# The FFN of two layers in four parts of 1024 of d_ff, written out, where it was two parts of 2048 in loops

## Time and profile before

| what | value |
| --- | --- |
| median of three runs | 2458.11 us (2457.42 to 2458.26) |
| span of the profiled execution | 2455.7 us |
| PE busy | 2437.2 us (99%) |
| DVE busy | 1321.1 us (54%) |
| ACT busy | 941.3 us (38%) |
| POOL busy | 292.5 us (12%) |
| DMA, mean | 106 GB/s |

### The profile page before, as it was taken

How to read it: one execution, slowest core, us unless ns; L and a number is a source line. 1 busy time by engine, 2 the same in 40 slices (tenths; PEclk the granted TensorE clock), 3 DMA queues, 4 the chain that set the end, 5 groups by cost and what they waited for, 6 DMA issues and landing times.

```text
span 2455.7 us, 31484 instructions
## 1 busy us (share of the span) xinstructions
PE 2437.2 (99%) x12348; PEld 1991.3 (81%) x12348; DVE 1321.1 (54%) x1761; ACT 941.3 (38%) x1359; POOL 292.5 (12%) x237
## 2 busy tenths in 40 slices
PE   9999999999999999999999999999999999999998
PEld 7877988889876888888988888877778788888886
DVE  7764732434966563243543437769995386343322
ACT  4345532333445453232432235532335554322321
POOL 1231000001122100000111123400000121111101
PEclk9999999999999999999999999999999999999999
DMA  4312222222231222222222235643342143222222
GB/s 165 142 44 69 86 103 103 86 103 103 78 129 35 103 86 100 89 103 94 79 103 102 93 103 174 206 164 116 142 149 83 63 152 129 100 88 102 78 98 81
DMA packets 46253, 259.64 MB, mean 106 GB/s; under 512 B 5504, under 2 KB 6016, under 8 KB 23232
## 3 DMA queue, kind: packets, MB, share of 16 engines
q1 hardware_dynamic: 43712, 248.42, 29.0%
q0 software_dynamic: 640, 5.51, 0.6%
q10 hardware_dynamic: 1792, 4.20, 0.5%
HBM read 240.27 MB, written 16.78 MB: 105 GB/s over the span
## 4 chain that ended last, share of the span: by engine, by line
PE 91%; DVE 6%; ACT 2%; issue 1%; DMA 0%; DVEq 0%; SPq 0%; ACTq 0%
PE gemm L451 74%; DVE out_sb L1599 2%; PE gemm L733 1%; DVE w_lo L401 1%; PE gemm L744 1%; PE gemm L735 1%; PE gemm L698 1%; PE gemm L699 1%; PE gemm L696 1%; PE turned L1135 1%; PE mixed L1147 1%; PE score L1124 1%; PE gemm L626 1%; PE gemm L627 1%; PE gemm L635 1%
## 5 line engine op out<-in xcount | busy, mean ns | idle before, releaser
L401 DVE TENSOR_TENSOR w_lo<-w_raw,w_hi 128x2048 fp32r<-128x2048 f32 (+2 forms) x207 | 439.2, 2122 | 480.7 <-ACT w_hi L393 480.3
L451 PE MATMUL gemm<-h_hi,w_hi 128*128 128x512 f32 x1744 | 691.2, 396 | 2.6 <-DVE w_lo L401 2.2
L451 PE MATMUL gemm<-h_hi,w_lo 128*128 128x512 f32 x1744 | 679.9, 390 | 0.0
L451 PE MATMUL gemm<-h_lo,w_hi 128*128 128x512 f32 x1744 | 679.2, 389 | 0.0
L393 ACT ACTIVATE w_hi<-w_raw 128x2048 fp32r<-128x2048 f32 (+3 forms) x217 | 381.9, 1760 | 345.5 <-PE gemm L451 302.8
L451 PEld LDWEIGHTS gemm<-h_hi,w_hi 128*128 128x128 f32 x1744 | 327.7, 188 | 81.8 <-issue 9.1
L451 PEld LDWEIGHTS gemm<-h_hi,w_lo 128*128 128x128 f32 x1744 | 327.3, 188 | 69.6
L451 PEld LDWEIGHTS gemm<-h_lo,w_hi 128*128 128x128 f32 x1744 | 327.8, 188 | 65.7 <-issue 1.0
L451 PE MATMUL gemm<-f_hi,w_hi 128*128 128x512 f32 x448 | 174.3, 389 | 0.0
L451 PE MATMUL gemm<-f_lo,w_hi 128*128 128x512 f32 x448 | 174.3, 389 | 0.0
L451 PE MATMUL gemm<-f_hi,w_lo 128*128 128x512 f32 x448 | 174.3, 389 | 0.0
(11 more groups left out here) (462 smaller groups left out, 3816.0 us busy)
## 6 DMA issues: line engine op xcount, KB each, us to landing
w_raw<-in_w SPq DMA_DIRECT2D x171, 1024.0 KB, 4.8
w_raw<-in_w SPq DMA_DIRECT2D x16, 768.0 KB, 4.2
w_raw<-in_w SPq DMA_DIRECT2D x16, 640.0 KB, 3.8
w_raw<-in_w SPq DMA_DIRECT2D x18, 512.0 KB, 3.6
trig_kept<-made SPq DMA_DIRECT2D x16, 512.0 KB, 5.7
trig<-trig_kept SPq DMA_DIRECT2D x16, 512.0 KB, 6.2
bias_t<-in_att_bias SPq DMA_DIRECT2D x2, 1536.0 KB, 8.1
decay_t<-in_c_decay SPq DMA_DIRECT2D x2, 1536.0 KB, 8.1
```

The costliest lines, as they stand in the source:

```text
L401: dve.tensor_tensor(flat(w_lo, b), flat(w_raw, b), flat(w_hi, b).bitcast(F32), ALU.subtract).then_inc(S["w_rest"], 1)
L451: mm = pe.matmul(dst, lhs, rhs, start=b.first and k == 0 and j == 0, stop=b.last and k == b.kt - 1 and j == 2)
```

## The change

The FFN goes in four parts of 1024 of d_ff: 4 up pieces, then 4 down pieces. `f_hi` and `f_lo` hold 8 tiles instead of 16. Each down output tile is one piece with a PSUM group of its own; the first part's 8 are copied to `out_sb` by ACT, those of the other three are added there by DVE (`added_down`). All loops of the FFN are written out. `last_in_halves` takes the one last piece instead of two. The spare place of the next block's second piece moves to memory that the smaller f buffers leave free. ACT's squares and scalings of tiles 0 to 5 now stand: 0 and 1 behind the rounding that follows the second down piece of the last part, 2 and 3 behind the one that follows the third, 4 and 5 right behind them.

Beside this some semaphores are merged: `wide_made` into `eps_made`, `half_read` and `y_s` into `y_read`, `t5_in` into `bc_in`, `x_back` into `time_in`, `ys_hi_s` into `y_hi_s`, with the waits counting on accordingly; DVE's `skip` in the second block no longer waits for its own two additions. Only the last of these is shown in the diff; the others change names and counts. Lines of the changed kernel in the first block's helpers are 2 lower than before (L870 becomes L868, L678 becomes L676).

```diff
-    for half in range(2):
-        for j in range(8):
-            out.append(Piece(0, half * 2048 + j * WCOLS, WCOLS, KD, "feat", "w_up"))
+    for part in range(D_FF // KB):
         for j in range(4):
-            for kb in range(2):
-                out.append(Piece(half * 2048 + kb * KB, j * WCOLS, WCOLS, KD, "feat", "w_down",
-                                 group=("down", half, j)))
+            out.append(Piece(0, part * KB + j * WCOLS, WCOLS, KD, "feat", "w_up"))
+        for j in range(4):
+            out.append(Piece(part * KB, j * WCOLS, WCOLS, KD, "feat", "w_down"))
     return out
...
-        for n in [lay * n1 + 18 for lay in range(DEPTH)] + [lay * n1 + 1 for lay in range(1, DEPTH + 1)]:
-            plan[n].spare = True
-        turns = [b for b in plan if not b.spare]
+        for lay in range(DEPTH):
+            plan[lay * n1 + 18].spare, plan[(lay + 1) * n1 + 1].spare = 0, 1
+        turns = [b for b in plan if b.spare is None]
...
-        spare_hi = at("spare_hi", [P, WSIZE], F32R, FZ)
-        spare_lo = at("spare_lo", [P, WSIZE], F32R, FZ + 8)
-        f_hi = at("f_hi", [P, 16, SEQ], F32R, FZ)
-        f_lo = at("f_lo", [P, 16, SEQ], F32R, FZ + 32)
+        spare_hi = [at("spare_hi", [P, WSIZE], F32R, FZ), at("spare_next_hi", [P, WSIZE], F32R, FZ + 32)]
+        spare_lo = [at("spare_lo", [P, WSIZE], F32R, FZ + 8), at("spare_next_lo", [P, WSIZE], F32R, FZ + 50.5)]
+        f_hi = at("f_hi", [P, KD, SEQ], F32R, FZ)
+        f_lo = at("f_lo", [P, KD, SEQ], F32R, FZ + 16)
...
-        UP = [17, 33]
-        DOWN = [25, 41]
+        PARTS = D_FF // KB
+        UP = [17 + 8 * part for part in range(PARTS)]
+        DOWN = [21 + 8 * part for part in range(PARTS)]
...
+            first = plan1[UP[0]]
+            opening_in_halves(pe, plan1[first.i:first.i + 2], 2 * lay, out_sb)
+            for b in plan1[first.i + 2:first.i + 4]:
+                product(pe, b, h_hi, h_lo, each=second_total(pe, 2 * lay, out_sb) if b.i == first.i + 2 else None)
+            for part in range(PARTS):
+                if part:
+                    for b in plan1[UP[part]:UP[part] + 4]:
                         product(pe, b, h_hi, h_lo)
-                with pe.Fori(1 - half, 3) as i:
-                    for b in plan1[first.i + 2:first.i + 4]:
-                        product(pe, b, h_hi, h_lo, Turn(i, dn=2, du=4, dt=4))
-                if half == 0:
-                    with pe.Fori(0, 2) as i:
-                        for b in plan1[DOWN[0]:DOWN[0] + 4]:
-                            product(pe, b, f_hi, f_lo, Turn(i, dn=4, du=8, dt=4),
-                                    tile_ready=(S["f_ready"], cnt("f_ready", 0)) if b.i < DOWN[0] + 2 else None)
-            for i in range(2):
-                for b in plan1[DOWN[1]:DOWN[1] + (2 if i else 4)]:
-                    product(pe, b, f_hi, f_lo, Turn(i, dn=4, du=8, dt=4),
-                            tile_ready=(S["f_ready"], cnt("f_ready", 16)) if i == 0 and b.i < DOWN[1] + 2 else None)
-            last_in_halves(pe, plan1[DOWN[1] + 6:DOWN[1] + 8], f_hi, f_lo, 2 * lay + 1, 6)
+                for j, b in enumerate(plan1[DOWN[part]:DOWN[part] + 4]):
+                    if part < PARTS - 1 or j < 3:
+                        product(pe, b, f_hi, f_lo,
+                                tile_ready=None if j else (S["f_ready"], cnt("f_ready", KD * part)))
+            last_in_halves(pe, [b], f_hi, f_lo, 2 * lay + 1, 6)
...
                 for m in range(2):
...
+            def copied_down(b, part):
+                for m in range(2):
+                    act.wait_ge(S["units"], b.u0 + m + 1)
+                    act.activation(out_sb[:, 2 * (b.i - DOWN[part]) + m, :], tile_of(b, m),
+                                   ACT.Copy).then_inc(S["g_free"], 1)
...
-            last_down = plan1[DOWN[1]].t0
-            for b in plan1[DOWN[1]:DOWN[1] + 7]:
+            for part in range(PARTS):
+                for b in plan1[UP[part]:UP[part] + 4]:
+                    opened = part == 0 and b.i < UP[0] + 2
+                    squared(b, part, opened)
+                    if not opened:
+                        round_block(act, b.n + 2)
+                downs = plan1[DOWN[part]:DOWN[part] + 4]
+                act.wait_ge(S["g_free"], downs[0].t0)
+                if part == PARTS - 1:
+                    break
+                for b in downs:
+                    if part == 0:
+                        copied_down(b, part)
+                    round_block(act, b.n + 2)
+            last_down = downs[0].t0
+
+            def scaled_squares(tiles):
+                norm_squares(act, out_sb, sq_f, wait=(S["g_free"], last_down), tiles=tiles, signal="half_square")
+                for q in tiles:
+                    act.activation(out_sb[:, q, :], out_sb[:, q, :], ACT.Copy,
+                                   scale=gains["mlp_post"][:, q:q + 1])
+
+            for j, b in enumerate(downs[:3]):
                 round_block(act, b.n + 2)
-                k = (b.i - DOWN[1]) // 2 * 2 - 2
-                if not b.last and k >= 0:
-                    norm_squares(act, out_sb, sq_f, wait=(S["g_free"], last_down), tiles=(k, k + 1),
-                                 signal="half_square")
-                    for q in (k, k + 1):
-                        act.activation(out_sb[:, q, :], out_sb[:, q, :], ACT.Copy,
-                                       scale=gains["mlp_post"][:, q:q + 1])
-            last = plan1[DOWN[1] + 7]
-            between_act(act, 2 * lay + 1, plan1[DOWN[1] + 6], last, plan[last.n + 1:last.n + 3], gains["mlp_post"],
+                if j:
+                    scaled_squares((2 * j - 2, 2 * j - 1))
+            scaled_squares((4, 5))
+            last = downs[3]
+            between_act(act, 2 * lay + 1, last, last, plan[last.n + 1:last.n + 3], gains["mlp_post"],
                         next_gain, sq_f, False)
...
+            def activated(b, part):
+
+                dve.wait_ge(S["g_free"], b.t0)
+                j = b.i - UP[part]
+                if part or j > 1:
+                    dve.wait_ge(S["f_ready"], cnt("f_ready", KD * part + 2 * j - 2))
...
+                for t in (2 * (b.i - UP[part]), 2 * (b.i - UP[part]) + 1):
+                    f_rest(t, part, tt[:, t % 4, :])
+
+            def f_rest(t, part, src):
+
+                dve.wait_ge(S["f_hi_s"], cnt("f_hi_s", KD * part + t + 1))
+                dve.tensor_tensor(f_lo[:, t, :], src, f_hi[:, t, :].bitcast(F32),
+                                  ALU.subtract).then_inc(S["f_ready"], 1)
+
+            def added_down(b, part):
+                dve.wait_ge(S["g_free"], b.t0)
                 for m in range(2):
-                    at_tile = i * 4 + (2 * j + m)
-                    dve.wait_ge(S["f_hi_s"], cnt("f_hi_s", 16 * half + i * 4 + (2 * j + m + 1)))
-                    dve.tensor_tensor(f_lo[:, at_tile, :], tt[:, 2 * j + m, :],
-                                      f_hi[:, at_tile, :].bitcast(F32), ALU.subtract).then_inc(S["f_ready"], 1)
+                    k = 2 * (b.i - DOWN[part]) + m
+                    dve.wait_ge(S["units"], b.u0 + m + 1)
+                    dve.tensor_tensor(out_sb[:, k, :], out_sb[:, k, :], tile_of(b, m), ALU.add).then_inc(S["g_free"], 1)
...
-            for b in plan1[DOWN[1]:DOWN[1] + 7]:
-                if b.last:
-                    for m in range(2):
-                        k = (b.i - DOWN[1]) // 2 * 2 + m
-                        dve.wait_ge(S["units"], b.u0 + m + 1)
-                        dve.tensor_tensor(out_sb[:, k, :], out_sb[:, k, :], tile_of(b, m),
-                                          ALU.add).then_inc(S["g_free"], 1)
+            activated_rest(first, 0)
+            activated_rest(second, 0)
+            for part in range(PARTS):
+                for b in plan1[UP[part]:UP[part] + 4]:
+                    if part or b.i > UP[0] + 1:
+                        activated(b, part)
+                        rest_block(dve, b.n + 2)
+                downs = plan1[DOWN[part]:DOWN[part] + 4]
+                if part == PARTS - 1:
+                    break
+                for b in downs:
+                    if part:
+                        added_down(b, part)
+                    rest_block(dve, b.n + 2)
+            for b in downs[:3]:
+                added_down(b, PARTS - 1)
                 rest_block(dve, b.n + 2)
-            group = plan1[DOWN[1] + 6]
-            last = plan1[DOWN[1] + 7]
-            between_dve(dve, 2 * lay + 1, group, last, plan[last.n + 1:last.n + 3], gains["mlp_post"], next_gain, sq_f,
+            last = downs[3]
+            between_dve(dve, 2 * lay + 1, last, last, plan[last.n + 1:last.n + 3], gains["mlp_post"], next_gain, sq_f,
...
                     add = dve.tensor_tensor(u_sb[to, a, :], u_sb[to, a, :], bank[3][src], ALU.add)
-                    add.then_inc(S["y_read"] if r else S["half_read"], 1)
-                dve.wait_ge(S["y_read"], a + 1)
-                dve.wait_ge(S["half_read"], a + 1)
```

(2 more changed lines are left out.)

134 lines of the change are left out of this document (42 added, 92 removed).

## The result

| | median of the runs | range |
| --- | --- | --- |
| before | 2458.05 us (20 runs) | 2457.19 to 2458.52 |
| after | 2462.27 us (20 runs) | 2460.26 to 2463.45 |

The ratio is 1.0017, with a 95% interval of 1.0010 to 1.0023: the changed kernel is 4.2 us slower, 0.17%, which by the bound of the prediction counts as no change. The forecast was 2461.7. That the two numbers lie 0.6 us apart is partly luck: one cost and one gain that were not in the sum, of 1.8 and 1.1 us, nearly cancel. They are the more instructive part of what follows. In both kernels the time of a run is 1.8 us above its span (2461.73 and 2459.9 in the profiled one after), not 2.4 as the prediction took from a profiled execution that was faster than the median; since only differences were added to the median, the forecast of 2461.7 does not hang on it.

The account below looks back on a forecast made before the run. PE, busy 99% of the span, was taken to bound the kernel. Terms -1.3 + 5.2 - 0.3 = +3.6 us on the 2458.11 us median gave 2461.7 us, 0.15% slower; range 2456.5 to 2465.5 us.

Parts of the forecast that it names:

- Term 1: Last down: one half-form piece becomes plain 512-column matmuls, gaining 0.63 us in each of two layers, -1.3 us.
- Term 2: Eight FFN switches from up to down: f tiles arrive in time with 1.2 us slack, so PE waits for nothing; cost 0.
- Term 3: Down sums in SBUF: 32 more DVE adds, 22 us of DVE work, hidden in idle stretches; cost 0.
- Term 4: End of last down: later squares and POOL's four adds delay the sum of squares by 2.6 us a layer, +5.2 us.
- Rival (a): Last down: POOL's adds finish in time, no new wait, only gains stay; 2456.5 us, chance 0.12.
- rival (b): Last down: POOL's adds take 2.16 us each, loss 4.1 us a layer; 2464.7 us, chance 0.10.
- Term 5: Last block: DVE four times no longer waits for its own two additions; -0.3 us, bounds 0 and -1.0.
- Rival (d): Behind the new 2.6 us stall PE's clock drops to half, losing 2.6 us more a layer; 2466.9 us, chance 0.08.
- Rival (c): Eight switches: weight subtractions slip ahead of f_lo's, making f halves 1.1 us late; 2470.5 us, chance 0.04.
- (e): Whole kernel: a gain over 4.9 us from a source the prediction could not name; chance 0.03.

Follow-up runs that it names:

- experiment 8: Kernel of experiment 1 with the second and third piece of each layer's last down made of 256-column products; 2458.04 us.
- experiment 1: Changed kernel with ACT's squares and scalings of tiles 0 to 5 each behind their own piece's rounding; 2455.37 us, ratio 0.9990.
- early_old_banks: Kernel of experiment 1 with the third block's PSUM banks dealt as before the change; 2455.37 us.
- Experiments 1 to 3: experiment 1; before_squares_late; and the changed kernel with squares and scalings of all six tiles behind the last rounding, 2467.82 us.
- before_squares_late: Kernel before, with ACT's squares and scalings of tiles 2 and 3 moved right ahead of those of 4 and 5; 2465.56 us.
- skip_waits_back: Changed kernel with DVE's wait for its own two additions and the signal behind it put back in skip; 2462.35 us.

## Why the prediction was right, and where it was not

- **Term 1, -1.3.** Right: -0.63 and -0.64 in the trace, and 0.67 a piece in experiment 8. The estimate of 0.1 from the Trainium skill ("TensorE: Matmul & The Clock Gate", section "Back-to-back issue gap") would have missed 1 us in both layers; the section gives that formula for an isolated matmul, and these are streams.
- **Term 2, nothing at the switches.** Right: one step of 0.2265 us over 1376 matmuls.
- **Term 3, nothing for the additions.** Right: DVE is 22.1 us busier, and experiment 1 has all additions and stands where the terms without them put it: 2458.0 - 1.3 - 0.45 - 1.0 = 2455.3, measured 2455.37 on the chip of that 2458.0 too (`early_old_banks`, the same but for the banks); beside its own runs of before, 2457.71, it is 0.4 us over the sum. The prediction's remark in this term that PE's matmuls keep their number is wrong against its own term 1: there are 96 fewer.
- **Term 4, +5.2.** Right, step by step: POOL R+9.67 for R+9.70, the sum R+10.71 for R+10.70, 2.62 a layer for 2.6. Experiments 1 to 3 undo it, make it in the kernel before, and lengthen it as worked out. Rival (a), no new wait, and rival (b), additions of 2.16 us, fall with it.
- **Term 5, -0.3.** Right in size (0.2 to 0.45). But the block gained 1.5. What the step left out is the fetch of PE's instructions. That it came out as a gain is luck: nothing in the change aims at it, and 64 more instructions take it away. I wrote of the loops that taking them away "gives nothing", since PE's step is the same in both; that is true of the loop and wrong of its code, which is longer and so moves every fetch behind it.
- **Rival (d), the clock, 0.08.** This is the chance that was most wrong. I took the wait of 1.4 us that leaves no mark as evidence for one of 2.5, and looked for the mark in slices of 61 us, in which half speed for 3.4 us costs under a tenth and cannot show: the page after reads 9 in all 40 as well, with a fall in it. In all 13 profiled executions of the study the wait of 1.4 us in mid-kernel indeed had no fall behind it, while of six waits of 2.5 us for the sum (`before_squares_late`, `skip_waits_back` and the changed kernel) four had one. The mechanism is real: it came in some executions and not in others, once or twice, at some 1.4 us each in the changed kernel in place of 2.6, and it added 2462.27 - 2460.5 = 1.8 us to the median. It should have been a term with a probability, not a rival.
- **Rival (c)** fell with term 2; (e) is what the instruction fetch might have been, in small.

The sum with the measured terms: 2458.05 - 1.3 + 5.2 - 0.4 - 1.0 = 2460.55 without a fall, where the six fastest runs lie (2460.3 to 2461.0); two falls of 1.4 make 2463.35, where the nine slowest lie (2462.8 to 2463.5). The 1.8 us is the median's distance from the first, so that the sum with it, 2462.35 against 2462.27, is no check of its own.

Open is what decides in an execution whether the clock falls behind a wait of 2.5 us; the same kernel shows both, in either layer.

## What to carry to other kernels

When a reduction over many tiles must be ready inside the last piece, its parts have to be made as soon as each exists: look at which instruction of the helper engine each part stands behind, and count the chain from the last release. A wait of PE costs more than its length once it is long enough for the clock to fall (here never behind 1.4 us, four times of six behind 2.5); price the fall as a probability, and look at the spread of the runs, not only at the median. And a gain or loss of about 1 us far from any edit can be the code's own length: compare the DMA view at that wait, look for the instruction queue's packet in it, and test with instructions that do nothing, before a reason is given to an edit.

## What was not expected of the hardware

- Instruction fetches take part in the DMA traffic: one packet of 16 KB, 1.0 to 1.6 us on one engine in the cases above, at the head of a transfer of 2 MB made that engine finish about 1 us after the other 15, and everybody waits for the last. 64 to 66 empty instructions on PE moved it in or out of the way, for 1.2 to 1.3 us of the whole kernel.
- Behind a wait of 2.5 us the granted clock fell to its lower level in the first layer and not in the second of one execution; behind 4.0 us it fell in both, and PE ran at half speed for 3.4 and 4.9 us. The fall can set in after PE has been back at full pace for 0.7 us. The Trainium skill ("TensorE: Matmul & The Clock Gate", section "What's actually happening") lets the gate fall after an idle stretch; the trace agrees that it does, and adds that one of 2.5 us is enough only sometimes.
- 18 products without use, put into a wait of 2.5 us, moved the sum by 0.05 us and kept the clock up in both layers of the profiled execution; the range of the runs went from 3.2 to 1.3 us.
